# Two transformer blocks on one core: linear attention of the mixed layers by chunks, some low weight parts on GpSimd, a second buffer for the last gate parts

## The chip, the cores and the metric

One core of one Trainium2 chip runs the whole program. The metric is the device time of one execution in microseconds (us); lower is better. The kernel is given as instructions for each engine: TensorE (PE in the profile), VectorE (DVE), ScalarE (ACT), GpSimd (POOL) and SyncE (SP), which wait for each other on semaphores.

## The reference

A first block of two layers is followed by a second of four. Both work on 256 tokens of width 1024 in float32. The change touches the first block's mixed layers, and the end of every feed-forward stage. A layer of the first block is, cut to what matters:

```
x = x + 0.5 * gt1 * swiglu(norm(x))            # d_ff 2816
proj = norm(x) @ mix_w_in                       # a_q a_k a_v | b_u | c_q c_k c_v c_r c_g
o_a = attention(rope(norm(a_q)), rope(norm(a_k)), a_v)     # 8 heads of 64, causal
o_b = silu(layernorm(conv31(a * sigmoid(g))))              # 256 channels
log_decay = log_sigmoid(c_g @ gla_gate_w + gla_gate_b) / 16
o_c = norm(gla(c_q, c_k, c_v, log_decay)) * silu(c_r)      # 4 heads of 64
x = x + gt2 * (concat(o_a, o_b, o_c) @ mix_w_out)
x = x + 0.5 * gt3 * swiglu(norm(x))

def gla(q, k, v, g):        # chunks of 64 tokens, G = cumsum of g inside a chunk
    q_t, k_t = q / 8 * exp(G), k * exp(-G)
    o_intra  = tril(q_t k_t^T) v
    k_end    = k * exp(G_last - G)
    state_n  = exp(G_last) * state_(n-1) + k_end^T v
    return o_intra + q_t state_(n-1)
```

## The kernel before

**Weights.** All weights pass through four slots (`SLOTS`) of 2048 floats per partition, in the order of one list, `plan.stream`. A unit is 256 columns of a weight matrix. SP loads it into `raw`. ACT rounds it to a high part `whi` (line 767) once TensorE has released the slot. DVE subtracts and makes the low part `wlo` (line 1187). TensorE then does 48 matmuls of 256 columns with it, three products for each of 16 tiles. `ahead(pos)` in ACT's and DVE's programs makes the parts up to three units ahead of the unit named. SP reloads `raw` of a slot when both `hi_done` and `lo_done` of its last unit have come, and its loads are one queue in the order of the list. `LO_ON_DVE` names all four slots, so GpSimd has a memset of `gate_w` (line 746) and nothing else.

**Mixed layer.** `mix1` has 13 units: c_r, c_g, c_k, c_q, the two of the convolution, two of mq, two of mk, c_v, two of mv; below they are units 0 to 12. In the first layer unit 0 is in slot 2, so the units in slot 3, the fourth, are 1, 5 and 9; in the second layer unit 0 is in slot 3, so they are 0, 4, 8 and 12. After unit 2 TensorE multiplies the gate weights (L2137). DVE takes the minimum with 0 (L1587), ACT takes abs, exp and log (L942 to L948), DVE subtracts (L1592). DVE then goes through the remaining units: it makes low parts, does the 62 taps of the convolution in lots of 10, 12, 12, 12 (L1560, L1563), normalizes queries and keys (`scaled`, L1493) and applies the rotation (`rope`, L1575 to L1579). TensorE's group sum for a norm stands behind a unit (L2106), its rotation matmul (L2209) two units later. Rotation b of DVE waits for TensorE's matmul, which waits for `scaled` of b.

**Head loop.** After the last rotation all engines go through steps j = 0 to 10. In step j TensorE computes the scores of head j (L2166, L2167), transposes the probabilities of head j-2 (L1880) and multiplies those of head j-3 with the values (L2125, L2126). DVE adds the mask and takes the row maxima of head j (L1632 to L1635), divides head j-1 (L1499 to L1643) and, in steps 4, 6, 8, 10, makes the low part of a pair of heads (L1649) once ACT has made the high part (L981). ACT does the exponentials (L930) and copies the transposed rows (L975). In the same steps linear attention goes up a tree of nine levels: DVE multiplies queries and keys by decays (`up`, L1508 to L1521), TensorE multiplies them (`level`, L2120), DVE keeps the entries that belong to the level (`keep_level`, L1538, L1542) in `c_A`. Steps 0 to 3 also hold the last 16 taps. Step 4 has the convolution's mean (L2188), step 6 its variance (L2192), steps 7 to 10 its root, silu and parts. Behind the loop TensorE multiplies `c_A` with c_v, ACT squares, TensorE sums (L2106), ACT takes the root, DVE scales and gates, ACT and DVE make the parts of tiles 6 and 7. The output projection (`outp`, L2426) waits, in its first unit, for each of the eight tiles of its input in turn.

**Feed-forward.** Eight stages of eleven steps. A step's gated product is split by ACT into `ghi` (L866) and by DVE into `glo` (L1403, or L1393 in the second block), and TensorE multiplies them with the output weights (L2058; those of the last step at L2091). There is one `ghi` and one `glo`:

```
if st.uses[O1] + j > 0:
    act.wait_ge(used[O1], st.uses[O1] + j)
f(ghi[:, :, :], product, ACT.Copy).then_inc(q["ffn_hi"], 1)
```

so ACT waits until TensorE has done the output products of the step before.

Of the kernel before, what the change touches and what calls it, by code (L numbers as in the profile page):

```python
# [29 lines left out]
P = 128  # L30
D = 1024
KT = D // P
S = 256
# [17 lines left out]
LO_ON_DVE = (0, 1, 2, 3)  # L51
# [183 lines left out]
def build(nc, a, out):  # L235

    ctx = ExitStack()
    with ctx:
# [51 lines left out]
        def work(at, *dims):  # L290
# [35 lines left out]
        c_g, conv_sig = conv_sq[:, 0:256], conv_y  # L326

# [35 lines left out]
            "level_mm level_up level_cp tree_mm tree_out tree_hi tree_lo "  # L363
            "lower_done mix_f sgu_v sgu_s sgu_mm sgu_hi sgu_lo final_x final_mm final_c out_done").split()}
# [3 lines left out]
        class Lane:  # L368
# [5 lines left out]

            def at(self, i, name):
                return self.sem, i * len(self.steps) + self.steps.index(name) + 1
# [3 lines left out]
                   "inv e0 e1 lb_a lb lb_rest")  # L380
        FIRST_ROWS = ("c", "ffn1_norm", "ada_b0")
# [49 lines left out]

        stages.append(Stage(kind="prologue"))
# [3 lines left out]
        for l in range(DEPTH1):  # L436
# [10 lines left out]
            last_use[0] = units[-1]  # L447
            stages.append(Stage(kind="mix1", l=l, units=units, last=units[-1], gn=take("gn", 5), heads=take("heads", 8),
                                masked=take("masked", 8), pairs=take("pairs", 4), tree=take("tree"),
                                rope=take("rope", 4)))  # L450
# [79 lines left out]
        n_stream = len(plan.stream)  # L530

# [55 lines left out]
        def mixer_tile(st, k):  # L587

            m = st.mixer
            if m.kind == "mix1":  # L590
                if k >= 6:
                    return q["tree_lo"], tree_base(m.tree) + 1
# [152 lines left out]
        def _(pool):  # L745
            nc.gpsimd.memset(gate_w[96:128, :, :], 0.0).then_inc(q["pro_s"], 1)
            for s, use, _, size in plan.stream:
                if s in LO_ON_DVE:
                    continue

                pool.wait_ge(hi_done[s], use + 1)
                if use > 0:
                    pool.wait_ge(used[s], use)
                nc.gpsimd.tensor_tensor(wlo[:, s, 0:size], raw[:, s, 0:size], whi[:, s, 0:size].bitcast(F32),
                                        ALU.subtract).then_inc(lo_done[s], 1)


        @block_.scalar
        def _(act):
# [173 lines left out]
            def mix1(st):  # L933
                us = st.units
                GA = 4 * st.l
                for n, u in enumerate(us):
                    take_out(u)
                    if n == 5:
# [11 lines left out]
                        f(c_f, gate_min, ACT.Exp, scale=1.0 / TAU).then_inc(q["gate_s"], 1)  # L950
# [11 lines left out]
                for j in range(8 + 3):  # L962
# [36 lines left out]
                act.wait_ge(q["tree_mm"], tree_base(st.tree) + 1)  # L999
                square(st.gn + 4, ps[:, 7, :], m_sq)  # L1000
                root(st.gn + 4, 4, HD, m_rs)
                act.wait_ge(q["tree_out"], tree_base(st.tree) + 1)
                f(hhi[:, 6:8, :], m_t[:, 0, :], ACT.Copy).then_inc(q["tree_hi"], 1)
# [172 lines left out]
        def _(dve):  # L1176
# [3 lines left out]
            def take_lo(s, use, size):  # L1180
                if s not in LO_ON_DVE:
                    return

# [183 lines left out]
            def ffn(st):  # L1367
                lo0 = STEPS * st.i
                A, B, _, O1 = st.slots
                for j in range(STEPS):  # L1370
                    pa, pb, o0, o1 = ffn_pos(st, j)
                    ahead(pb if st.defer is None else pa)
                    if st.defer is not None:
# [19 lines left out]
                        tt(glo[:, :, :], product, ghi[:, :, :].bitcast(F32), ALU.subtract).then_inc(q["ffn_lo"], 1)  # L1393
# [9 lines left out]
                    tt(glo[:, :, :], product, ghi[:, :, :].bitcast(F32), ALU.subtract).then_inc(q["ffn_lo"], 1)  # L1403
# [141 lines left out]
            def mix1(st):  # L1545
# [34 lines left out]

                for n, u in enumerate(us):
                    take_out(u)
                    if n == 4:
# [877 lines left out]
```

## Time and profile before

| | us |
|---|---|
| three runs | 2851.28, 2853.35, 2855.09 |
| median | 2853.35 |
| the profiled execution's own time | 2852.6 |
| its span, first to last instruction | 2850.8 |
| TensorE busy in the span | 2707.0 (95%) |
| VectorE busy | 1890.2 (66%) |
| ScalarE busy | 1343.5 (47%) |
| GpSimd busy | 0.7 |
| granted TensorE clock, mean | 0.976 |

Busy time is a sum over the span; the wait that a change removes or adds is found where one engine stands and another works. For this kernel these are the two mixed layers (about 290 to 433 and 860 to 1003 us of the span) and the ends of the eight feed-forward stages. A granted clock of 0.5 is 1.2 GHz and one of 1.0 is 2.4 GHz.

### The profile page before, as it was taken

How to read it: one execution, taken by the hardware profiler on the slowest of the kernel's cores; microseconds unless marked ns; L12 is line 12 of the kernel's file. 1: busy time of each engine (PE TensorE's matmuls, PEld its weight loads, DVE VectorE, ACT ScalarE, POOL GpSimd, SP SyncE). 2: the span in 40 equal slices, each digit the busy share in tenths (PEclk: the TensorE clock that was granted, in tenths of full speed). 3: DMA queues.
4: the chain of work that ended last, by engine and by line, in shares of the span. 5: the costliest groups of instructions: out<-in, count | busy, mean ns of one | idle time of the engine just before them, and what ended most of it. 6: DMA issues, size and time to landing. Idle time of an engine off the chain costs nothing.

```text
span 2850.8 us, 53332 instructions
## 1 busy us (share of the span) xinstructions
PE 2707.0 (95%) x22439; PEld 2628.3 (92%) x22439; DVE 1890.2 (66%) x2639; ACT 1343.5 (47%) x1576; POOL 0.7 (0%) x5
## 2 busy tenths in 40 slices
PE   6799979999999799999999999999999999999998
PEld 6799959999999599999999999999999999999998
DVE  5877786877777855576565666656566555775564
ACT  3334634435446354465544535544465544555443
POOL 0000000000000000000000000000000000000000
PEclk8899979999999799999999999999999999999999
DMA  8988505997985045664355643535665266643552
GB/s 238 310 287 276 170 27 185 296 291 266 290 287 172 21 144 196 206 193 149 104 200 184 197 152 109 163 133 193 206 206 178 104 207 199 201 147 118 178 192 103
DMA packets 458802, 533.07 MB, mean 187 GB/s; under 512 B 9879, under 2 KB 435081, under 8 KB 458633
## 3 DMA queue, kind: packets, MB, share of 16 engines
q1 hardware_dynamic: 457340, 530.11, 56.9%
q8 instruction: 113, 1.85, 0.3%
q10 hardware_dynamic: 1293, 0.65, 0.1%
q14 instruction: 56, 0.46, 0.0%
HBM read 528.10 MB, written 2.62 MB: 186 GB/s over the span
## 4 chain that ended last, share of the span: by engine, by line
PE 79%; DVE 10%; DMA 3%; issue 3%; ACT 3%; SPq 1%; ACTq 0%; DVEq 0%
PE ps L2058 13%; PE ps L1889 11%; PE ps L1890 11%; PE ps L1891 11%; PE ps L1907 10%; PE ps L2426 8%; DMA work<-in_ada_w 3%; DVE work L1291 2%; DVE wlo L1187 2%; PE ps L2091 2%; DVE work L1563 2%; PE ps L2120 1%; PE ps L2236 1%; PE ps L2238 1%; PE ps L2237 1%
## 5 line engine op out<-in xcount | busy, mean ns | idle before, releaser
L1187 DVE TENSOR_TENSOR wlo<-raw,whi 128x2048 fp32r<-128x2048 f32 (+1 forms) x514 | 975.8, 1919 | 410.2 <-ACT whi L767 410.0
L767 ACT ACTIVATE whi<-raw 128x2048 fp32r<-128x2048 f32 (+1 forms) x514 | 826.4, 1615 | 436.5 <-PE ps L1891 148.0
L1889 PE MATMUL ps<-hhi,whi 128*128 128x256 f32 x1600 | 451.4, 282 | 13.8 <-issue 11.1
L1890 PE MATMUL ps<-hlo,whi 128*128 128x256 f32 x1600 | 445.0, 278 | 0.0
L1891 PE MATMUL ps<-hhi,wlo 128*128 128x256 f32 x1600 | 444.4, 278 | 0.0
L1889 PE MATMUL ps<-parts_f,whi 128*128 128x256 f32 x1344 | 372.6, 277 | 7.8 <-issue 7.8
L1890 PE MATMUL ps<-parts_f,whi 128*128 128x256 f32 x1344 | 371.5, 276 | 0.0
L1891 PE MATMUL ps<-parts_f,wlo 128*128 128x256 f32 x1344 | 371.2, 276 | 0.0
L2058 PE MATMUL ps<-ghi,whi 128*128 128x256 f32 x1280 | 355.5, 278 | 7.1 <-DVE wlo L1187 7.0
L2058 PE MATMUL ps<-glo,whi 128*128 128x256 f32 x1280 | 355.2, 278 | 0.0
L2058 PE MATMUL ps<-ghi,wlo 128*128 128x256 f32 x1280 | 354.9, 277 | 0.0
L1889 PEld LDWEIGHTS ps<-hhi,whi 128*128 128x128 f32 x1600 | 303.2, 190 | 18.0 <-issue 18.0
L1890 PEld LDWEIGHTS ps<-hlo,whi 128*128 128x128 f32 x1600 | 303.4, 190 | 0.7 <-issue 0.7
L1891 PEld LDWEIGHTS ps<-hhi,wlo 128*128 128x128 f32 x1600 | 302.9, 189 | 0.0
L1889 PEld LDWEIGHTS ps<-parts_f,whi 128*128 128x128 f32 x1344 | 252.3, 188 | 9.3 <-issue 9.2
L1890 PEld LDWEIGHTS ps<-parts_f,whi 128*128 128x128 f32 x1344 | 252.3, 188 | 0.1
L1891 PEld LDWEIGHTS ps<-parts_f,wlo 128*128 128x128 f32 x1344 | 252.3, 188 | 0.0
L2058 PEld LDWEIGHTS ps<-ghi,whi 128*128 128x128 f32 x1280 | 241.5, 189 | 8.2 <-issue 8.2
L2058 PEld LDWEIGHTS ps<-glo,whi 128*128 128x128 f32 x1280 | 241.5, 189 | 0.0
L2058 PEld LDWEIGHTS ps<-ghi,wlo 128*128 128x128 f32 x1280 | 241.4, 189 | 0.0
L1291 DVE SCALAR_TENSOR_TENSOR work<-work,silu_c 128x256 f32<-128x256 f32 x490 | 197.0, 479 | 0.0
L1907 PE MATMUL ps<-hhi,whi 128*128 128x256 f32 x880 | 177.5, 284 | 16.2 <-DVE hlo L1352 16.2
(277 smaller groups left out, 4892.0 us busy)
## 6 DMA issues: line engine op xcount, KB each, us to landing
raw<-in_ffn_w_in SPq DMA_DIRECT2D x88, 1024.0 KB, 10.6
raw<-in_ffn_w_gu SPq DMA_DIRECT2D x88, 1024.0 KB, 5.1
work<-in_ada_w SPq DMA_DIRECT2D x72, 1024.0 KB, 8.9
raw<-in_ffn_w_out SPq DMA_DIRECT2D x88, 512.0 KB, 6.0
raw<-in_ffn_w_down SPq DMA_DIRECT2D x88, 512.0 KB, 5.4
raw<-in_ca_w_kv SPq DMA_DIRECT2D x32, 1024.0 KB, 5.8
raw<-in_mix_w_in SPq DMA_DIRECT2D x24, 1024.0 KB, 6.3
raw<-in_da_w_in SPq DMA_DIRECT2D x24, 1024.0 KB, 6.0
```

The lines of the kernel that those rows point to most:

```text
L767: f(whi[:, s, 0:size], raw[:, s, 0:size], ACT.Copy).then_inc(hi_done[s], 1)
L1187: tt(wlo[:, s, 0:size], raw[:, s, 0:size], whi[:, s, 0:size].bitcast(F32), ALU.subtract).then_inc(lo_done[s], 1)
L1291: m = stt(acc, w, silu_c[:, k:k + 1], acc, ALU.mult, ALU.add)
L1563: m = stt(conv_acc[:, t, :], h, w, conv_acc[:, t, :], ALU.mult, ALU.add)
L1889: mm(dst, wh, xh, start=first, stop=False)
L1890: mm(dst, wh, xl, start=False, stop=False)
L1891: return mm(dst, wl, xh, start=False, stop=last)
L1907: o = mm(ps[:, slot, 256 * m:256 * m + 256], w[:, k, P * m:P * m + P], x_[:, k, :], start=k == 0 and i == 0 and m == 0, stop=k == KT - 1 a ...
L2058: o = mm(dst, a_, b_[:, t, :], start=first and t == 0 and i == 0 and m % 2 == 0, stop=False, skip_group_check=True)
L2091: o = mm(dst, a_, b_[:, t, :], start=False, stop=t == 1 and i == 2 and m % 2 == 1, skip_group_check=True)
L2120: o = mm(d[:, c], K[rows_, tile, c], Q[rows_, tile, c], start=True, stop=True)
L2426: o = mm(ps[:, bank, 256 * m:256 * m + 256], w[:, k, P * m:P * m + P], x_[:, k, :], start=k == 0 and i == 0 and m == 0, stop=k == KT - 1 a ...
```

## The change

Linear attention in `mix1` no longer uses the tree. DVE makes three masks out of constants (five small operations, in `rstd`), sums the log decays inside chunks of 64 tokens with two scans, and ACT takes exp of the sums and of their negatives (one more exp than before). DVE multiplies queries and keys (three operations of 128x512 and one small copy in `decayed`; two of 128x128 in `far`). TensorE multiplies in three rounds (`gla_level` 0, 1, 2) in steps 0, 1, 2 of the head loop, in place of nine, and DVE keeps what belongs in `c_A` in the same steps. `c_A` is cleared by GpSimd first. The product with c_v moves to step 4, the square to ACT's step 5, the group sum to TensorE's step 6, the root to ACT's step 7, scaling and gating to DVE's step 8; the parts of tiles 6 and 7 come last. The second block's tree (`hgrn`) is as before but for the numbering of its semaphore.

GpSimd makes the low parts of the units that `mix1` has in slot 3. The gate parts of the last step of each feed-forward stage go to `parts_f`, and ACT does not wait for TensorE there.

```diff
-LO_ON_DVE = (0, 1, 2, 3)
+POOL_SLOT = 3
...
+        gate_sum, decay_in, growth_in, k_end = c_f, gate_abs, gate_min, c_f
+        reset, intra = rstd[:, 1, :], rstd[:, 0, 0:P]
+        decay = stat[:, :, 12:16]
...
+        GLA = Lane("gla_v", "ones reset below within intra sums q_in k_in decay k_end q_far k_far")
...
+            pool_units.append([u for u in units if u.slot == POOL_SLOT])
...
+        def gate_parts(j):
+
+            return (ghi[:, :, :], glo[:, :, :]) if j < STEPS - 1 else (fhi[:, 0:2, :], flo[:, 0:2, :])
...
+            for l in range(DEPTH1):
+                for n, u in enumerate(pool_units[l]):
+                    take_lo(u.slot, u.use, KT * u.cols)
+                    if n == 1:
+                        pool.wait_ge(*GLA.at(l, "k_end"))
+                        nc.gpsimd.memset(c_A, 0.0).then_inc(q["gla_zero"], 1)
...
-                    if st.uses[O1] + j > 0:
+                    if j < STEPS - 1 and st.uses[O1] + j > 0:
                         act.wait_ge(used[O1], st.uses[O1] + j)
-                    f(ghi[:, :, :], product, ACT.Copy).then_inc(q["ffn_hi"], 1)
+                    f(gate_parts(j)[0], product, ACT.Copy).then_inc(q["ffn_hi"], 1)
...
-                        f(c_f, gate_min, ACT.Exp, scale=1.0 / TAU).then_inc(q["gate_s"], 1)
+                        act.wait_ge(*GLA.at(st.l, "sums"))
+                        f(decay_in, gate_sum, ACT.Exp, scale=1.0 / TAU).then_inc(q["gla_s"], 1)
+                        f(growth_in, gate_sum, ACT.Exp, scale=-1.0 / TAU).then_inc(q["gla_s"], 1)
...
                     if j == 5:
+                        act.wait_ge(q["gla_tokens"], st.l + 1)
+                        square(st.gn + 4, ps[:, 1, :], m_sq)
...
                     if j == 7:
+                        root(st.gn + 4, 2, HD, m_rs)
...
+                def decayed():
+
+                    dve.wait_ge(q["gla_s"], 2 * l + 2)
+                    for u in us[2:4]:
+                        dve.wait_ge(*bank_read(u))
+                    tt(c_q, c_q, decay_in, ALU.mult).then_inc(*GLA.step)
+                    tt(c_k, c_k, growth_in, ALU.mult).then_inc(*GLA.step)
+                    v.tensor_copy(decay, decay_in[:, :, HD - 1::HD]).then_inc(*GLA.step)
+                    dve.wait_ge(*GLA.at(l, "k_in"))
+                    last = chunks(decay_in)[:, :, HD - 1:HD].broadcast_to([P, 8, HD])
+                    tt(chunks(k_end), chunks(c_k), last, ALU.mult).then_inc(*GLA.step)
...
+                    if n == 1:
+                        masks()
+                    if n == 6:
+                        decayed()
...
+                        for t in range(2):
+                            m = v.tensor_tensor_scan(gate_sum[:, t, :], reset, gate_min[:, t, :], 0.0, ALU.mult, ALU.add)
+                        m.then_inc(*GLA.step)
...
-                    if j < LEVELS:
-                        keep_level(st.tree, j, c_A, 4, source)
+                    if j < 3:
+                        keep(j)
+                    if j == 1:
+                        far()
...
-                        level(st.tree, j, c_q, c_k, 4, dst, part)
+                    if j < 3:
+                        gla_level(j)
                     if j == 4:
+                        gla_tokens()
```

Three places show how the instructions now stand. First VectorE in the second mixed layer, from the end of the gates to the first rotation; `work` holds all activations of the stage. Before:

```order
L1592 TENSOR_TENSOR work<-work 128x512
L1187 TENSOR_TENSOR wlo<-raw,whi 128x2048
L1594 MEMSET work 128x2x30
L1597 TENSOR_TENSOR work<-ps,work 128x2x256
L1560 TENSOR_SCALAR work<-work,taps,vec 128x256 x2
L1563 SCALAR_TENSOR_TENSOR work<-work,taps 128x256 x8
L1187 TENSOR_TENSOR wlo<-raw,whi 128x2048 x3
L1493 SCALAR_TENSOR_TENSOR work<-ps,lam,work 128x512
L1563 SCALAR_TENSOR_TENSOR work<-work,taps 128x256 x12
L1187 TENSOR_TENSOR wlo<-raw,whi 128x2048
```

Now:

```order
L1675 TENSOR_TENSOR work<-work 128x512
L1679 SCALAR_TENSOR_TENSOR work<-rstd,work 128x256 x2
L1682 MEMSET work 128x2x30
L1685 TENSOR_TENSOR work<-ps,work 128x2x256
L1583 TENSOR_SCALAR work<-work,taps,vec 128x256 x2
L1586 SCALAR_TENSOR_TENSOR work<-work,taps 128x256 x8
L1208 TENSOR_TENSOR wlo<-raw,whi 128x2048
L1625 TENSOR_TENSOR work<-work 128x512
L1626 TENSOR_TENSOR work<-work 128x512
L1627 COPY stat<-work 128x2x4
L1630 TENSOR_TENSOR work<-work 128x512
L1208 TENSOR_TENSOR wlo<-raw,whi 128x2048 x2
```

The scans (L1679) and the four operations of `decayed` (L1625 to L1630, the last is k_end) have come in, and two low parts, of units 8 and 12, have left this stretch.

Second, GpSimd from its old memset on, both layers:

```order
L761 MEMSET gate_w 32x512
L767 ISA
L767 TENSOR_TENSOR wlo<-raw,whi 128x1024
L767 TENSOR_TENSOR wlo<-raw,whi 128x2048
L775 MEMSET work 128x1536
L767 TENSOR_TENSOR wlo<-raw,whi 128x2048 x3
L775 MEMSET work 128x1536
L767 TENSOR_TENSOR wlo<-raw,whi 128x2048 x2
```

The memset of `c_A`, which waits for k_end, stands ahead of the low part of unit 9 in the first layer and ahead of those of units 8 and 12 in the second.

Third, TensorE in step 4 of the head loop, after the scores, with the products of head 1's values, then of c_v, then the convolution's mean (L2290):

```order
L2206 MATMUL ps<-work 64x256
L2207 MATMUL ps<-work 64x128
L2206 MATMUL ps<-work 64x256
L2207 MATMUL ps<-work 64x128
L2206 MATMUL ps<-work 64x256
L2207 MATMUL ps<-work 64x128
L2206 MATMUL ps<-work 64x256
L2207 MATMUL ps<-work 64x128
L2206 MATMUL ps<-work 64x256
L2207 MATMUL ps<-work 64x128
L2290 MATMUL ps<-work,con 128x512
```

The last four pairs ahead of L2290 are those of c_v, which stood behind the whole loop before.

## Rows read from the trace of the kernel before

**Rows 1.** Page, part 1: busy time, share of the span, instructions

```profile
PE 2707.0 (95%) x22439; PEld 2628.3 (92%) x22439; DVE 1890.2 (66%) x2639; ACT 1343.5 (47%) x1576; POOL 0.7 (0%) x5
```

**Rows 2.** Busy time by stretch: PE, PEld, DVE, ACT, POOL, PEclk, DMA share, GB/s

```profile
322.00:371.00 49.00, 42.51 (x321) 38.12 (x320) 48.07 (x75) 22.79 (x22) 0.00 (x0) 0.97 0.47 151
371.00:432.00 61.00, 46.19 (x283) 32.98 (x283) 45.75 (x134) 22.11 (x57) 0.00 (x0) 0.75 0.00 1
...
941.00:1000.00 59.00, 45.02 (x270) 32.55 (x271) 44.69 (x133) 21.75 (x57) 0.00 (x0) 0.74 0.00 1
```

**Rows 3.** Waits of TensorE, 942 to 1003 us: total us, times, longest; line 2120

```profile
PE ps L2120 <- DVE work L1518: 7.2, 6, 1.9
```

**Rows 4.** Waits of TensorE over the whole span, those of line 2091

```profile
PE ps L2091 <- DVE glo L1393: 6.0, 4, 1.5
PE ps L2091 <- DVE glo L1403: 3.7, 4, 1.5
```

**Rows 5.** Timeline, end of the fourth feed-forward stage: start, us, engine, [idle before]

```profile
1202.54 0.63 ACT L866 ACTIVATE ghi<-work 128x512 fp32r<-128x512 f32 x1 [4.39 <-PE ps L2058]
...
1203.95 0.38 PE L2091 MATMUL ps<-ghi,whi 128*128 128x256 f32 x1 [1.51 <-DVE glo L1403]
```

**Rows 6.** Timeline of DVE in the second mixed layer, after the gates

```profile
892.01 0.69 DVE L1592 TENSOR_TENSOR work<-work 128x512 f32<-128x512 f32 x1 [9.63 <-ACT work L948]
892.62 2.29 DVE L1187 TENSOR_TENSOR wlo<-raw,whi 128x2048 fp32r<-128x2048 f32 x1
894.87 0.11 DVE L1594 MEMSET work<- 128x60 f32 x1
...
899.38 6.70 DVE L1187 TENSOR_TENSOR wlo<-raw,whi 128x2048 fp32r<-128x2048 f32 x3
```

**Rows 7.** The instructions that write the gate weights: min/median/max ns, first and last start

```profile
L746 POOL MEMSET gate_w<- x1: 520/520/520, 0.7 to 0.7; 32x512 f32 x1
```

**Rows 8.** Timeline of PE and DVE around the first rotation, second mixed layer

```profile
898.43 1.02 PE L2106 MATMUL ps<-work,con 128*128 128x512 f32 x2
...
912.03 1.02 PE L2209 MATMUL ps<-work,con 128*128 128x512 f32 x2
...
914.26 0.70 DVE L1575 TENSOR_TENSOR work<-ps,cs 128x512 f32<-128x512 f32 x1
```

**Rows 9.** The same in the first mixed layer

```profile
335.58 1.02 PE L2106 MATMUL ps<-work,con 128*128 128x512 f32 x2
...
342.82 1.02 PE L2209 MATMUL ps<-work,con 128*128 128x512 f32 x2
...
345.03 0.69 DVE L1575 TENSOR_TENSOR work<-ps,cs 128x512 f32<-128x512 f32 x1
```

**Rows 10.** Timeline of DVE in the head loop, first mixed layer

```profile
373.85 0.56 DVE L1632 TENSOR_TENSOR work<-ps,con 128x384 f32<-128x384 f32 x1 [1.80 <-PE ps L2167]
...
381.71 1.44 DVE L1542 COPY_PREDICATED work<-con,ps 128x256 f32<-128x256 int32 x4 [0.62 <-PE ps L2120]
383.05 1.66 DVE L1563 SCALAR_TENSOR_TENSOR work<-work,taps 128x256 f32<-128x256 f32 x4
...
397.72 0.55 DVE L1632 TENSOR_TENSOR work<-ps,con 128x384 f32<-128x384 f32 x1
...
399.23 0.35 DVE L1643 TENSOR_SCALAR work<-work,stat 128x256 f32<-128x256 f32 x1
...
421.88 0.87 DVE L1662 SCALAR_TENSOR_TENSOR work<-work,vec 128x256 f32<-128x256 f32 x2
```

**Rows 11.** Timeline of PE in the loop and behind it, first mixed layer

```profile
399.79 2.07 PE L2188 MATMUL ps<-work,con 128*128 128x512 f32 x2
...
426.48 1.13 PE L2106 MATMUL ps<-work,con 128*128 128x512 f32 x2 [2.83 <-ACT work L916]
...
431.96 0.51 PE L2426 MATMUL ps<-hhi,whi 128*128 128x256 f32 x2 [0.25 <-DVE hlo L1675]
```

**Rows 12.** Stretch in which the second output projection starts (columns as in rows 2)

```profile
995.00:999.00 4.00, 4.00 (x18) 3.49 (x18) 1.73 (x3) 1.41 (x3) 0.00 (x0) 0.59 0.01 4
```

More of the change, by code:

```diff
@@ L373, in __init__, with step @@
                 self.sem, self.steps = q[name], steps.split()
+            @property
+            def step(self):
+                return self.sem, 1
             def at(self, i, name):
@@ L530, in build @@
         n_stream = len(plan.stream)
+        on_pool = {(u.slot, u.use) for units in pool_units for u in units}
         def all_read(units):
@@ L746, in _, with take_lo @@
             nc.gpsimd.memset(gate_w[96:128, :, :], 0.0).then_inc(q["pro_s"], 1)
-            for s, use, _, size in plan.stream:
-                if s in LO_ON_DVE:
-                    continue
+            def take_lo(s, use, size):
                 pool.wait_ge(hi_done[s], use + 1)
@@ L934, in mix1 @@
                 us = st.units
[L935 removed]
+                GA = 3 * st.l
                 for n, u in enumerate(us):
@@ L997, in mix1 @@
                         f(hhi[:, 4:6, :], conv_y, ACT.Copy).then_inc(q["conv_hi"], 1)
[L999 to L1003, printed above, removed]
+                act.wait_ge(q["gla_out"], st.l + 1)
+                f(hhi[:, 6:8, :], m_t[:, 0, :], ACT.Copy).then_inc(q["gla_hi"], 1)
             def diff(st):
@@ L1180, in take_lo @@
             def take_lo(s, use, size):
-                if s not in LO_ON_DVE:
+                if (s, use) in on_pool:
                     return
@@ L1579, in rope, with masks @@
                     tt(dst, rows2(t), rows2(m_rope), ALU.add).then_inc(q["rope_done"], 1)
+                def masks():
+                    tril = const("tril")
+                    v.memset(rstd[:, 1, :], 1.0).then_inc(*GLA.step)
+                    dve.wait_ge(*GLA.at(l, "ones"))
+                    v.memset(rstd[:, 1, 0::HD], 0.0).then_inc(*GLA.step)
+                    tt(intra, block, tril, ALU.mult).then_inc(*GLA.step)
+                    dve.wait_ge(*GLA.at(l, "below"))
+                    tt(intra, block, intra, ALU.subtract).then_inc(*GLA.step)
+                    dve.wait_ge(*GLA.at(l, "within"))
+                    tt(intra, intra, ident, ALU.add).then_inc(*GLA.step)
@@ new lines, in far, with keep @@
+                def far():
+                    dve.wait_ge(q["gla_mm"], 3 * l + 2)
+                    dve.wait_ge(*GLA.at(l, "k_end"))
+                    tt(c_q[:, :, 3 * HD:], c_q[:, :, 3 * HD:], decay[:, :, 2:3].broadcast_to([P, 2, HD]), ALU.mult)\
+                        .then_inc(*GLA.step)
+                    tt(k_end[:, :, 0:HD], k_end[:, :, 0:HD], decay[:, :, 1:2].broadcast_to([P, 2, HD]), ALU.mult)\
+                        .then_inc(*GLA.step)
+                def keep(L):
+                    dve.wait_ge(q["gla_mm"], 3 * l + L + 1)
+                    if L:
+                        dve.wait_ge(q["gla_cp"], 3 * l + L)
+                    else:
+                        dve.wait_ge(q["gla_zero"], l + 1)
+                        dve.wait_ge(*GLA.at(l, "intra"))
+                    far_level = const("level")[:, 6 * P:7 * P]
+                    for h in range(4):
+                        src = ps[:, (1, 2)[h % 2], 256 * (h // 2):256 * (h // 2) + 256]
+                        if L == 2:
+                            m = v.tensor_copy(c_A[:, h, P:2 * P], src[:, 0:P])
+                            continue
+                        dst = c_A[:, h, :].rearrange("p (c t) -> p c t", c=3)[:, 0::2, :]
+                        mask = (intra, far_level)[L].bitcast(I32).unsqueeze(1).broadcast_to([P, 2, P])
+                        m = v.copy_predicated(dst, mask, rows2(src))
+                    m.then_inc(q["gla_cp"], 1)
```

85 lines of the change are left out of this document (48 added, 37 removed).

## The prediction

> **What bounds the kernel now.** I read the busy shares first: TensorE is busy 2707 of 2850.8 us [rows 1], so some 144 us of standing still are all that a change of order can win, and only where TensorE stands. The busy time by stretch then shows where. In the mixed layers' unit stretch DVE is busy 48.07 of 49 us while TensorE is at 42.5; in the head loop behind it TensorE is busy 46.2 of 61 us, and its clock is granted at 0.75, a mix of the two levels [rows 2]. The reader is to see that DVE sets the pace in both. TensorE's waits name what ends last in the loop: the levels of the tree wait for DVE's multiplication of the keys (L1518), 7.2 us in one layer [rows 3]. The same view of the whole span has one more regular wait, at the last gate parts: 6.0 + 3.7 us over the eight feed-forward stages [rows 4]. About 0.2%, 5.7 us, is what a measurement of this kernel can tell from no change.
>
> **The change part by part.**
>
> *Last gate parts.* TensorE ends a stage's tenth output products, ACT then rounds (0.63), DVE subtracts (0.69), and TensorE has stood 1.51 us [rows 5]. With a second buffer both are done while TensorE works on the tenth step's outputs. The product is there by then, since it needs only the last input products. The eight waits are 9.7 us [rows 4]; where low parts or ada sums occupy DVE before, the shorter wait shows it. The next thing late is the low part of the last output unit, which DVE has made before those waits end. **-9.7**, bounds -7 and -9.7.
>
> *Gates to k_end, on DVE.* Second layer: the subtraction starts at 892.01 and ends 0.69 later, 892.7 [rows 6]. Two scans of 256: no row has one. Bounds are 0.4 each (a tap, a quarter of 1.66 [rows 10]) and twice that; I take 0.6, since each element waits for the one before: 893.9. The low part of unit 8 (2.2) goes to GpSimd. Memset, gating and ten taps are 894.87 to 899.38 [rows 6], 4.5: 898.4. Low part of unit 9, 2.2: 900.6. Three multiplications at 0.6 (the 0.69 of rows 6 less overlap) and a copy, 2.1: **k_end at 902.7**. First layer: the subtraction starts at 322.8 (as far ahead of the rotation, 345.03 less 914.26 - 892.01, [rows 8, 9]) and unit 8's low part is still on DVE: k_end at 333.5. ACT's extra exp (0.63) is covered by DVE's gating and taps, and the five mask operations stand where DVE idles 9.63 us ahead of the subtraction [rows 6].
>
> *GpSimd.* Behind k_end comes the memset of 1536 elements. The only row is 512 elements in 0.52 us [rows 7]: 1.5 us. Then the low part that TensorE wants next. A subtraction on GpSimd has no row. Lower bound 2.29, DVE's own time [rows 6]; upper bound 6.3, two reads and a write of 2048 each at the memset's pace of 1 ns. I take the middle, **4.3**. So unit 8 of the second layer has its low part at 902.7 + 1.5 + 4.3 = 908.5, and unit 9 of the first at 333.5 + 5.8 = 339.3. (The Trainium skill, GPSIMD Engine Reference, Elementwise side-by-side cycle accounting, gives 4497 ns for this size against 2293 ns on VectorE; by its figure each layer would be 0.2 us later. The trace agrees on VectorE's.) The earlier units in slot 3 are made long before their use, in DVE's idle time.
>
> *What that wait does.* TensorE wants unit 8 when the group sum of 898.43 is through, at 899.0, so it stands 9.5 us. From there the rotation ends at 913.05 and DVE uses it at 914.26 [rows 8]. After the stall the clock starts low; I add 1.6, what the 4 us at 0.59 in rows 12 lose. The rotation ends at 913.05 + 9.5 + 1.6 = 924.2, so DVE's chain is **9.9 late**. It was the chain that ended last, and the low part of unit 12 that it no longer makes stood before this point, so it gives nothing back. First layer: unit 9 is wanted at 336.2, the stall is 3.1, the rotation of 343.84 comes at 346.9, against 345.03 [rows 9]: **1.9 late**; DVE by itself (+1.2 scans, +2.1 multiplications, -2.2 for unit 9) would be 1.1 late. Queued behind: SP's load of the next slot-3 unit waits for GpSimd, and three loads behind it. They have over 12 us until TensorE frees their slots, with DMA at 0.47 [rows 2]; nothing.
>
> *Head loop, first layer as the example.* Steps 0 to 3 ran from 373.85 to 397.72, 23.9 us [rows 10]. DVE now has in them a softmax part of 1.86 (397.72 to 399.58) three times and 1.2 once, 6.8; four lots of taps at 1.66, 6.6; two keeps at 1.44 and one of half that, 3.6 [rows 10]; two small multiplications, 0.6: 17.6, **-6.3**. TensorE's share is shorter. Steps 4 to 8, 397.72 to 421.88, 24.2 us, were not paced by DVE alone, but by the round from probabilities over TensorE and ACT to the pair's low part. Gone are five levels with their waits, 5 of the 7.2 us [rows 3]. New on TensorE are c_v's products and the group sum. The mean's product, 512 columns, is 2.07 at the low clock [rows 11], so the group sum is 2.1 and c_v's 1536 columns 3.1 to 6.2; lower if a pair's heads run side by side, which I take. New on ACT are a square and a root, 1.9. That is 7.1 against 5 and the levels' own matmuls: **0**, bounds -6 and +7. Behind step 8 the time from 421.88 to 431.96 plus two tiles of 0.68 was 11.4 [rows 10, 11], with the group sum waiting 2.83 for ACT. Now it is the convolution's scale, silu, table, parts, then five tiles: 0.9 + 0.9 + 1.3 + 0.6 + 0.4 + 0.4, some 4.9 with waits, + 3.4 + 1.6 for a low clock [rows 12] = 9.9, **-1.5**. Sum -7.8; for the waits between engines I take **-7 a layer**, bounds -3 and -10.
>
> *Sum.* -9.7 + 1.9 + 9.9 - 14 = -11.9. The profiled execution took 2852.6, its span being 2850.8; that gives 2840.7. The median stands 0.75 above that execution: **2841.5 us**.
>
> **Rivals.**
>
> *DVE held (2847).* While GpSimd subtracts, DVE's own operations with two inputs in SBUF stand. No row shows the two engines working together, so bounds are nothing and a whole GpSimd instruction. In the first layer GpSimd's 4.3 us fall on low parts and taps, so the chain is 5.6 late, not 1.9: +3.7. In the second the subtraction of unit 8 waits for one of DVE's (+0.7) and that of unit 12 takes DVE up to 1.5 more: +2. Against it: most of its time in the second layer DVE would wait for TensorE anyway. (The Trainium skill, SBUF, Who interferes with whom, states this rule: a VectorE instruction with two SBUF inputs and a GpSimd one that reads SBUF exclude each other for the whole instruction. The trace has nothing to weigh it.)
>
> *GpSimd starved: slower (2863).* The same exclusion, but DVE's queue is never empty (48.07 of 49 us [rows 2]) and keeps going first. GpSimd starts only where DVE stops, at the first rotation. First layer: DVE has 12.7 us of work after 333.5 (three low parts at 2.2, twelve taps 4.8, two scalings 1.3), so 346.2 + 4.3, unit 9 at 350.5, rotation at 350.5 + 7.6 + 1.6 = 359.7, 14.7 late. Second (two low parts): 913.3 + 4.3 = 917.6, rotation 14.1 + 1.6 later, 933.3, 19.0 late. Together 33.7 in place of 11.8: +21.9. It turns the sign when GpSimd starts over 9 us late in each layer.
>
> *Low clock throughout (2850).* With less for TensorE in the loop the clock may stay at 1.2 GHz for steps 4 to 8 and the projection. Only about 3 a layer would be left: +8. For it: 0.75 and 0.74 now [rows 2]. Against: the matmuls of steps 2 to 5 close up.
>
> *The gate parts bring nothing (2851).* If the low part of the last output unit, or DVE's ada sums, end as late: +9.7.
>
> *The stall is not there (2833).* A memset and a subtraction at DVE's pace, 3 us together, give back 2.8 in the second layer and 1 in the first, and with DVE short of work the loop may give 10: -9 in all.
>
> **How the numbers follow.** Forecast 0.42, held 0.25, low clock 0.10, starved 0.10, gates nothing 0.07, no stall 0.06. Faster by over 0.2% means below 2847.6: nearly all of the forecast (0.39), over half of held (0.14), a little of low clock (0.02), all of no stall: 0.61. Slower is starved: 0.10. Same: 0.29. The range leaves out starved and half of no stall: 2834 to 2851, which also takes in the bounds of the scan, the subtraction and the loop.
>
> **What would show it.** Eight gaps before the last outputs (L2091's successor) shrink from 1.5 to near zero. TensorE waits once for GpSimd's `wlo`, 9 to 10 us in the second mixed layer and about 3 in the first. The GpSimd subtraction reads 4 to 5 us. From the first rotation to the loop nothing changes; steps 0 to 3 take 17 to 18 us, steps 4 to 8 about 24. DVE's taps and low parts keep their 0.4 and 2.29 us; if one of them reads 4 us or more, DVE was held. Wrong would be a GpSimd subtraction that starts over 5 us after its memset, or a loop with no shorter steps.

## The result and the profile after

The changed kernel takes **2837.99 us** (median of 4 runs, 2835.5 to 2838.6) against 2854.22 for the kernel before on the same chip (4 runs): ratio 0.994, 95% interval 0.9924 to 0.9956. The forecast was 2841.5 in 2834 to 2851, so the sign held and the time lies 3.5 us below it. The profiled execution took 2838.55 us and its span is 2836.7, 14.1 less than before; the forecast's sum was -11.9.

The page's busy times, against [rows 1]: TensorE 9.3 us less, DVE 15.6 less, GpSimd 35.6 in place of 0.7.

```profile
PE 2697.7 (95%) x22247; PEld 2615.3 (92%) x22247; DVE 1874.6 (66%) x2568; ACT 1343.6 (47%) x1578; POOL 35.6 (1%) x14
```

I laid the two traces side by side at the first operation of each norm. The span's 14.1 us come from: -1.9 in the start, +2.3 in the first feed-forward stage, **-5.4 in the first mixed layer**, +1.1 and -2.6 in the next two feed-forward stages, **+3.0 in the second mixed layer**, **-9.4 in the five later feed-forward stages** (-1.96, -1.79, -2.06, -1.81, -1.78), and -1.1 spread over the rest. The first two are no work of the change: other kernels below, which differ little up to there, stand anywhere from 3.0 us ahead of the kernel before (kernel 3, end of the start) to 3.2 behind it (kernel 9, end of the first stage).

Within the mixed layers the same marks in both kernels, taken from the timelines (us; "rotation" is the first use of a rotated head pair on DVE, L1575 before and L1598 after):

| stretch | before, layer 1 / 2 | after, layer 1 / 2 | difference | forecast |
|---|---|---|---|---|
| norm to gate subtraction | 40.19 / 40.22 | 39.38 / 40.16 | -0.8 / -0.1 | 0 |
| gate subtraction to first rotation | 22.24 / 22.25 | 27.61 / 32.70 | **+5.4 / +10.4** | +1.9 / +9.9 |
| first rotation to step 0 | 28.82 / 28.98 | 28.80 / 28.91 | 0 / -0.1 | 0 |
| steps 0 to 3 | 23.87 / 23.83 | 17.35 / 17.36 | **-6.5 / -6.5** | -6.3 |
| step 4 to the convolution's scale | 24.16 / 23.10 | 24.22 / 25.15 | +0.1 / +2.1 | 0 |
| from there to the next norm | 31.54 / 32.67 | 28.08 / 29.73 | **-3.5 / -2.9** | -1.5 |

**GpSimd.** Its timeline around the gates, first layer and then second:

```profile
299.96 4.79 POOL L767 TENSOR_TENSOR wlo<-raw,whi 128x2048 fp32r<-128x2048 f32 x1 [22.65 <-ACT whi L787]
333.04 1.39 POOL L775 MEMSET work<- 128x1536 f32 x1 [28.29 <-DVE work L1630]
334.39 5.20 POOL L767 TENSOR_TENSOR wlo<-raw,whi 128x2048 fp32r<-128x2048 f32 x1
...
896.10 1.38 POOL L775 MEMSET work<- 128x1536 f32 x1 [31.29 <-DVE work L1630]
897.44 5.16 POOL L767 TENSOR_TENSOR wlo<-raw,whi 128x2048 fp32r<-128x2048 f32 x1
```

DVE in the same places:

```profile
300.62 4.29 DVE L1610 TENSOR_TENSOR rstd<-con 128x128 f32<-128x128 f32 x1
...
332.29 0.69 DVE L1630 TENSOR_TENSOR work<-work 128x512 f32<-128x512 f32 x1
332.90 8.84 DVE L1208 TENSOR_TENSOR wlo<-raw,whi 128x2048 fp32r<-128x2048 f32 x2
...
349.93 0.67 DVE L1598 TENSOR_TENSOR work<-ps,cs 128x512 f32<-128x512 f32 x1
...
859.40 0.28 DVE L1610 TENSOR_TENSOR rstd<-con 128x128 f32<-128x128 f32 x1
...
885.36 0.69 DVE L1675 TENSOR_TENSOR work<-work 128x512 f32<-128x512 f32 x1 [9.63 <-ACT work L968]
886.08 1.27 DVE L1679 TENSOR_TENSOR_SCAN work<-rstd,work 128x256 f32<-128x256 f32 x2
...
895.35 0.69 DVE L1630 TENSOR_TENSOR work<-work 128x512 f32<-128x512 f32 x1
895.96 8.78 DVE L1208 TENSOR_TENSOR wlo<-raw,whi 128x2048 fp32r<-128x2048 f32 x2
...
918.06 0.69 DVE L1598 TENSOR_TENSOR work<-ps,cs 128x512 f32<-128x512 f32 x1 [4.02 <-PE ps L2304]
```

The reader is to see L1610 twice: 0.28 us where GpSimd is idle, 4.29 where GpSimd subtracts; and two low parts at 8.8 us that take 4.5 elsewhere. DVE was held. The order can be read too: GpSimd's subtraction takes 4.60 us when alone, but 5.16 to 5.20 behind DVE's low part. It waits for the running one (895.96 + 2.2 = 898.2, less 897.44), works 4.6 us, which together is 0.2 more than was read, and DVE's next starts when it is done. Each lets the other in after one instruction, so neither starves.

TensorE's timeline at the two units in question, first layer and then second:

```profile
336.19 1.02 PE L2187 MATMUL ps<-work,con 128*128 128x512 f32 x2
339.69 0.77 PE L1987 MATMUL ps<-hhi,whi 128*128 128x256 f32 x2 [2.47 <-issue]
...
892.84 1.10 PE L2187 MATMUL ps<-work,con 128*128 128x512 f32 x2 [0.91 <-ACT work L936]
902.70 0.76 PE L1987 MATMUL ps<-hhi,whi 128*128 128x256 f32 x2 [8.76 <-issue]
```

Both resume 0.1 us behind the end of GpSimd's subtraction (334.39 + 5.20, 897.44 + 5.16), though the view calls the wait "issue".

**The loop.** The stretches of the loop (columns as in [rows 2]): the first layer's steps 0 to 3 and its steps 4 to 8, then the second layer's:

```profile
378.73:396.08 17.35, 15.18 (x73) 10.43 (x74) 16.44 (x52) 5.42 (x19) 0.00 (x0) 0.50 0.00 1
396.08:420.30 24.22, 18.25 (x77) 9.78 (x73) 9.47 (x32) 10.76 (x31) 0.00 (x0) 0.83 0.00 0
...
946.97:964.33 17.36, 15.18 (x73) 10.43 (x74) 16.44 (x51) 5.41 (x19) 0.00 (x0) 0.50 0.00 1
964.33:989.48 25.15, 21.09 (x77) 11.15 (x73) 9.47 (x32) 10.77 (x31) 0.00 (x0) 0.67 0.00 0
```

DVE works 16.4 of the 17.4 us of steps 0 to 3 and stands for 15 of 25 us behind them. Steps 4 to 8 took longer where the granted clock stayed low: 0.67 and 25.2 us, against 0.83 and 24.2.

**The gate parts.** TensorE's waits at the last outputs are gone: in none of the eight stages does it stand before them. At the end of the fourth feed-forward stage, where it stood 1.51 us [rows 5], its timeline now reads:

```profile
1198.42 0.28 PE L2138 MATMUL ps<-ghi,wlo 128*128 128x256 f32 x1
1198.54 0.39 PE L2172 MATMUL ps<-parts_f,whi 128*128 128x256 f32 x2
```

DVE's timeline there in the kernel before (the last gate product is the first row):

```profile
1197.08 0.69 DVE L1400 TENSOR_TENSOR work<-work,ps 128x512 f32<-128x512 f32 x1 [2.69 <-PE ps L1891]
...
1205.01 2.29 DVE L1187 TENSOR_TENSOR wlo<-raw,whi 128x2048 fp32r<-128x2048 f32 x1 [1.11 <-ACT whi L767]
...
1207.42 3.23 DVE L1438 SCALAR_TENSOR_TENSOR x<-ps,scale_out,x 128x256 f32<-128x256 f32 x8
```

The same in the changed kernel:

```profile
1193.34 0.69 DVE L1422 TENSOR_TENSOR work<-work,ps 128x512 f32<-128x512 f32 x1 [2.69 <-PE ps L1971]
...
1198.03 2.29 DVE L1208 TENSOR_TENSOR wlo<-raw,whi 128x2048 fp32r<-128x2048 f32 x1 [1.77 <-ACT whi L787]
...
1200.44 1.89 DVE L1461 SCALAR_TENSOR_TENSOR x<-ps,scale_out,x 128x256 f32<-128x256 f32 x4
1202.82 0.88 DVE L1461 SCALAR_TENSOR_TENSOR x<-ps,scale_out,x 128x256 f32<-128x256 f32 x2 [0.48 <-PE ps L2172]
1204.18 0.88 DVE L1461 SCALAR_TENSOR_TENSOR x<-ps,scale_out,x 128x256 f32<-128x256 f32 x2 [0.48 <-PE ps L2172]
```

Before, all eight updates of x ran back to back: they were late, behind a low part that was late because ACT rounded its unit only after the gate parts (1202.54 in [rows 5]). Now the last four wait for TensorE. From gate product to last update it was 1210.65 - 1197.08 = 13.57 us, and is 1205.06 - 1193.34 = 11.72: 1.85 won, not 1.51.

### The profile page after: what moved, and what is told of

Its sections match the earlier page's. It is cut to its first block, busy times and chain, and to the rows that moved or that the text cites. A ratio compares the mean times of both kernels' runs of the same rounds, so it can differ in the third digit from the quotient of the medians.

```text
span 2836.7 us, 52845 instructions
## 1 busy us (share of the span) xinstructions
PE 2697.7 (95%) x22247; PEld 2615.3 (92%) x22247; DVE 1874.6 (66%) x2568; ACT 1343.6 (47%) x1578; POOL 35.6 (1%) x14
## 4 chain that ended last, share of the span: by engine, by line
PE 81%; DVE 8%; DMA 4%; issue 3%; ACT 3%; SPq 0%; ACTq 0%; DVEq 0%
PE ps L2138 14%; PE ps L1969 12%; PE ps L1970 11%; PE ps L1971 11%; PE ps L1987 10%; PE ps L2522 8%; DMA work<-in_ada_w 2%; DVE work L1312 2%; DVE wlo L1208 2%; PE ps L2172 2%; PE ps L2331 1%; PE ps L2333 1%; PE ps L2332 1%; DMA bias_rows<-raw 1%; DVE work L1586 1%
## 5 line engine op out<-in xcount | busy, mean ns | idle before, releaser
L1969 PE MATMUL ps<-hhi,whi 128*128 128x256 f32 x1600 | 452.1, 283 | 16.2 <-issue 14.2
L1987 PE MATMUL ps<-hhi,whi 128*128 128x256 f32 x880 | 178.9, 285 | 27.5 <-DVE hlo L1373 16.3
```

What stands on the lines that cost most here:

```text
L1969: mm(dst, wh, xh, start=first, stop=False)
L1987: o = mm(ps[:, slot, 256 * m:256 * m + 256], w[:, k, P * m:P * m + P], x_[:, k, :], start=k == 0 and i == 0 and m == 0, stop=k == KT - 1 a ...
```

## The experiments

All are compared with the kernel before, run beside them on the same chip. Stretches are from each kernel's profiled execution.

**1. The gate parts alone.** The kernel before with the second buffer:

```diff
+ def gate_parts(j): return (ghi, glo) if j < STEPS - 1 else (fhi[:, 0:2, :], flo[:, 0:2, :])
- if st.uses[O1] + j > 0:
+ if j < STEPS - 1 and st.uses[O1] + j > 0:
      act.wait_ge(used[O1], st.uses[O1] + j)
- f(ghi[:, :, :], product, ACT.Copy).then_inc(q["ffn_hi"], 1)
+ f(gate_parts(j)[0], product, ACT.Copy).then_inc(q["ffn_hi"], 1)
...
```

> The kernel before with the second buffer for the last gate parts and nothing else. Theory Q (the queue behind): in the fourth feed-forward stage the time from the last gate product on DVE to the last update of x fell from 13.57 us (1197.08 to 1210.65) to 11.72 us (1193.34 to 1205.06), 1.85 and not 1.51, because ACT's rounding of the gate parts no longer delays the two weight units behind it, whose low part stands in DVE's queue ahead of the updates of x. Eight stages at 1.85: -14.8, about 2839.4. Rival W (only TensorE's waits, as forecast): -9.7, about 2844.5. A third, that stages with ada sums gain less than the others because DVE is busy there anyway: between 2840 and 2846 with the later five at 1.8 to 2.0 and the first three below 1.

Measured: 2843.71 us (2836.7 to 2846.12) against 2854.96, ratio 0.9956 (0.9941 to 0.997): -11.3. The five later feed-forward stages gave -1.93, -1.78, -2.05, -1.81 and -2.03; the fourth as much as in the changed kernel. Of the three stages with ada sums (TensorE's products with `in_ada_w`, which make `mods`) the second gave -0.8 and the third -0.1; over eight of the profiles with the second buffer (kernels 1, 2, 4, 7 to 10 and the changed kernel) they average 0.0 and -1.6, against +0.2 and -0.3 in the one other kernel without it. The first can't be told from the start's variation. By the total (the interval is -8.6 to -16.8 us) W and the third theory can't be told apart; by the stages the third holds for the five later ones, 1.9 each. What the first three give is known less well: some 1 to 1.6 us in the second and third together, on average all of it in the third.

One more thing stands in this profile. Its tree is the old one, and yet steps 4 to 8 of its head loop took 28.24 us in the first layer and 22.25 in the second, where the kernel before took 24.16 and 23.10 (columns as in [rows 2]):

```profile
395.90:424.14 28.24, 25.54 (x127) 16.48 (x127) 19.06 (x64) 9.32 (x28) 0.00 (x0) 0.64 0.00 1
970.47:992.72 22.25, 16.82 (x127) 11.01 (x127) 18.78 (x63) 9.43 (x28) 0.00 (x0) 1.00 0.00 1
```

So the same instructions took 6 us more in one layer than in the other, at a lower granted clock.

**2. All low parts on DVE.**

```diff
- pool_units.append([u for u in units if u.slot == POOL_SLOT])
+ pool_units.append([])
...
```

GpSimd's memset of the score tile stays; with no units left it stands alone.

> The changed kernel with every low part on DVE; GpSimd keeps only the memset of the score tile. Theory G (GpSimd's low parts are late themselves and hold DVE): the first rotation comes 22.2 + 1.3 (scans) + 2.1 (multiplications) = 25.6 us behind the gate subtraction in both layers, against 27.6 and 32.7 in the changed kernel, so -2.0 and -7.1: about 2829. DVE's mask multiplication reads 0.28 us in both layers and two low parts 4.5. Rival L (the loop sets the time and takes back what comes earlier, by a lower clock or the later rotation): less than 3 us faster, 2835 to 2838. Rival D (DVE's three low parts more per layer, 6.9 us, fall on the chain): 2 to 7 us slower than the changed kernel.

Measured: **2829.03 us** (2826.91 to 2832.24), ratio 0.9911 (0.9894 to 0.9929). Gate subtraction to rotation is 25.45 and 25.46 us, where 25.6 was expected. The mask multiplication reads 0.28, two low parts 4.49. GpSimd's part in the change was a loss of 2.2 and 7.2 us ahead of the rotation. Rivals L and D fall.

**3. Linear attention by chunks alone.** Kernel 2 with the last gate parts in the old buffer.

> Linear attention by chunks alone: low parts all on DVE, last gate parts in the one buffer as before. By parts against the kernel before: +3.4 a layer ahead of the first rotation (scans 1.3, multiplications 2.1), -6.3 in the loop's steps 0 to 3, 0 in steps 4 to 8, -1.5 (forecast) to -3.4 (read in the changed kernel's first layer) behind it: -8.8 to -12.6 for two layers, 2841.5 to 2845.5. With theory Q it should stand 14.8 above low_on_dve, with W 9.7. A rival in which the earlier rotation only makes a longer wait in the loop: 2849 or more.

Measured: 2838.68 us (2834.07 to 2844.18), ratio 0.9946 (0.9926 to 0.9966): -16.3, more than the sum by parts. In its profile the two mixed layers give -7.6 and -7.0, the start -3.0 and the first feed-forward stage +1.6. Stretches: rotation at 25.46 in both layers, steps 0 to 3 17.4, steps 4 to 8 22.0 and 24.0, then 28.1 twice (before 31.5 and 32.7): the sum by parts is passed behind the loop and, by 2 us, in steps 4 to 8 of the first layer. It stands 9.7 above kernel 2. That is W's number, but not by W's parts: in the two profiles the five later stages alone differ by 9.7. With the 11.3 of kernel 1 that makes some 10 us for the gate parts.

**4. The memset behind the third low part.**

```diff
- if n == 1:
+ if n == 2:
      pool.wait_ge(*GLA.at(l, "k_end"))
      nc.gpsimd.memset(c_A, 0.0).then_inc(q["gla_zero"], 1)
```

> The changed kernel with one line moved: GpSimd makes its third low part of a layer as soon as ACT has rounded the unit, and the memset of the score tile, which waits for the decayed keys, comes behind it and not ahead. It tells the late start from the hold. Theory G: TensorE's stall of 8.76 us in the second layer is gone, DVE is still held for 4.3 us, so its chain is 25.6 - 2.3 (a low part less) + 4.3 = 27.6 us long in both layers, against 27.6 and 32.7: -5, about 2833. If the hold cost nothing, 23.3 in both: -4.3 and -9.4, about 2824. If the late start cost nothing (the hold alone): no change, 2838. In the trace one of DVE's operations with two inputs beside GpSimd's subtraction should read 4 us more than its usual time.

Measured: 2830.43 us (2825.87 to 2834.36), ratio 0.9914 (0.9895 to 0.9934). GpSimd's timeline around the gates:

```profile
327.31 4.59 POOL L767 TENSOR_TENSOR wlo<-raw,whi 128x2048 fp32r<-128x2048 f32 x1 [23.52 <-ACT whi L787]
...
875.27 4.62 POOL L767 TENSOR_TENSOR wlo<-raw,whi 128x2048 fp32r<-128x2048 f32 x1 [12.16 <-ACT whi L787]
...
899.13 4.82 POOL L767 TENSOR_TENSOR wlo<-raw,whi 128x2048 fp32r<-128x2048 f32 x1 [4.06 <-ACT whi L787]
```

DVE's operations beside the first and the last of them:

```profile
327.00 5.05 DVE L1583 TENSOR_SCALAR work<-work,taps,vec 128x256 f32<-128x256 f32 x2
...
898.60 9.20 DVE L1586 SCALAR_TENSOR_TENSOR work<-work,taps 128x256 f32<-128x256 f32 x12
```

This run parts the two mechanisms. In the first layer the part is made in time for TensorE, yet the rotation comes at 27.58 us, as in the changed kernel: there the hold alone is the cost (two taps 5.05 us in place of 0.74). In the second the late start was: the part is now made at 875.27, while DVE stands ahead of the gates, the stall is gone, and the rotation comes at 25.45, not 32.70 nor my 27.6. I had not seen that the part falls into DVE's idle time; of two low parts less (-4.5) and one hold (+4.4, twelve taps 9.20 in place of 4.83) nothing is left.

**5 and 6. What in GpSimd's instruction holds DVE.** Its subtraction is replaced. In place of the fourth slot's low part kernel 5 has a copy of the whole unit and kernel 6 zeros, so neither computes what the kernel should; they are for the timelines alone.

```diff
- nc.gpsimd.tensor_tensor(wlo[:, s, 0:size], raw[:, s, 0:size], whi[:, s, 0:size].bitcast(F32), ALU.subtract)
+ nc.gpsimd.tensor_copy(wlo[:, s, 0:size], raw[:, s, 0:size])
```

in kernel 5, and in kernel 6

```diff
+ nc.gpsimd.memset(wlo[:, s, 0:size].bitcast(F32), 0.0)
```

> The changed kernel with GpSimd's subtraction replaced by a copy of the unit (one input from SBUF in place of two; the low parts of the fourth slot are left out of the products). Theory R (what holds DVE is that GpSimd reads SBUF while DVE has two inputs there): DVE is still held, for as long as the copy takes; the mask multiplication in the first layer (0.28 us by itself, 4.29 beside the subtraction) reads over 1 us, and one of the two low parts behind the decayed keys waits for the copy's whole length. Theory T (only a GpSimd instruction with two inputs holds): 0.28 us and 4.5 us for the two.

> The changed kernel with GpSimd's subtraction replaced by a memset of the same 2048 elements (nothing read; the low parts of the fourth slot are left out). Theory R: DVE is not held; the mask multiplication reads 0.28 us in both layers and the two low parts behind the decayed keys 4.5 us. A rival in which any GpSimd access of SBUF holds DVE: some of them read 1.5 to 2 us more. The memset of 1536 elements took 1.38 us, so 2048 should take 1.8; TensorE's stall at the third unit of the second layer falls by 3 to 7 us, from 8.76, the rest being the wait for the decayed keys.

Kernel 5 (2837.09 us, one run), GpSimd's timeline:

```profile
302.13 2.11 POOL L767 CAST wlo<-raw 128x2048 fp32r<-128x2048 f32 x1 [22.82 <-ACT whi L786]
...
336.61 2.57 POOL L767 CAST wlo<-raw 128x2048 fp32r<-128x2048 f32 x1
```

DVE's in the same places:

```profile
302.80 1.58 DVE L1609 TENSOR_TENSOR rstd<-con 128x128 f32<-128x128 f32 x1
...
335.13 6.19 DVE L1207 TENSOR_TENSOR wlo<-raw,whi 128x2048 fp32r<-128x2048 f32 x2
```

Kernel 6 (2827.44 us, one run), GpSimd's timeline:

```profile
299.63 1.81 POOL L767 MEMSET wlo<- 128x2048 f32 x1 [24.92 <-ACT whi L786]
...
334.07 1.83 POOL L767 MEMSET wlo<- 128x2048 f32 x1
```

And DVE's:

```profile
300.31 0.29 DVE L1609 TENSOR_TENSOR rstd<-con 128x128 f32<-128x128 f32 x1
...
332.60 4.49 DVE L1207 TENSOR_TENSOR wlo<-raw,whi 128x2048 fp32r<-128x2048 f32 x2
```

For DVE's operations with two inputs theory R holds: a copy of 1.9 us holds the next one (+1.3, +1.7 us), a memset of 1.8 us over the same time does not (0.29, 4.49). It is GpSimd's read that counts there, one input being enough. In kernel 6 the first rotation of the first layer stands at 23.3 us. In the second it is at 29.3: the unit is released only at 890.24 + 1.81, since the memset of the score tile still waits for the decayed keys. That is the late start without any hold.

**7. GpSimd only where DVE is idle.** The fourth slot's first two units of the first layer, its first three of the second, the memset behind them.

```diff
- pool_units.append([u for u in units if u.slot == POOL_SLOT])
+ pool_units.append([u for u in units if u.slot == POOL_SLOT][:2 + l])
```

> GpSimd makes low parts only where DVE stands idle: the first two units of the fourth slot in both layers and the third of the second layer (ahead of the gates), the memset behind them; the rest on DVE. Theory G: TensorE never waits for GpSimd, DVE has one low part less (2.3 us) between the gates and the first rotation of the second layer, 23.2 us against 25.5 with all of them on DVE, and 25.5 in the first: 2 us faster than low_on_dve. Rival L (what comes earlier is lost in the loop): the same as low_on_dve within 1 us.

Measured: 2824.77 us (2823.46 to 2826.12), ratio 0.9901 (0.9884 to 0.9918). Rotations at 25.47 and 23.29 us, as expected. That 2.2 us shows in the profile; the ratio's interval overlaps kernel 2's, so by their times the two can't be told apart.

**8. The linear attention three steps later.** Kernel 2 with the decayed keys out of the unit stretch:

```diff
- if n == 6:
-     decayed()
...
- if j < 3:
-     keep(j)
+ if j == 2:
+     decayed()
+ if 3 <= j < 6:
+     keep(j - 3)
...
```

> low_on_dve with the linear attention three steps later in the head loop: decayed keys at DVE's step 2 and not in the unit stretch, levels at steps 3, 4 and 5, the sum over tokens at 6, square at 7, root at 8, gating at 9. DVE works without a pause from the gates to step 4 and then stands for 16 of 25 us, so what crosses step 4 (keeps 1.44 + 0.7, two small multiplications 0.6: 2.7 us) is won if DVE sets the pace up to step 4 and has slack behind it: 25.5 + 28.8 + 17.4 = 71.7 us from the gate subtraction to step 4 become 69.0, and steps 4 to 8 stay at 22 to 25 us: 5 us faster than low_on_dve over two layers. Rival P (behind step 4 TensorE is the bound, busy 21.2 of 25.3 us at a granted clock of 0.66, and the level products now fall there): 69.0 all the same, but steps 4 to 8 3 us longer: no change.

Measured: **2817.70 us** (2814.49 to 2818.17), ratio **0.9872** (0.9852 to 0.9893), 20 us below the changed kernel. Steps 0 to 3 and 4 to 8 of the first layer's loop as windows (columns as in [rows 2]), kernel 2:

```profile
375.00:392.36 17.36, 13.89 (x73) 9.60 (x74) 16.45 (x52) 5.42 (x19) 0.00 (x0) 0.60 0.00 1
392.36:417.72 25.36, 21.27 (x76) 11.24 (x73) 9.47 (x32) 10.75 (x31) 0.00 (x0) 0.66 0.00 0
```

Kernel 8:

```profile
374.05:390.07 16.02, 11.84 (x62) 7.88 (x61) 15.77 (x45) 5.42 (x19) 1.38 (x1) 0.61 0.00 1
390.07:411.70 21.63, 15.89 (x79) 9.06 (x80) 11.81 (x42) 9.92 (x29) 0.00 (x0) 0.89 0.00 0
```

Gate subtraction to step 4 fell from 71.6 to 68.4 us (expected 69.0), since DVE sets that pace: 6.5 us over two layers. Steps 4 to 8 fell too, from 25.4 and 23.9 to 21.6 and 22.0, in the first layer at a granted clock of 0.89 in place of 0.66, TensorE doing more matmuls (79 against 76) in less busy time. Rival P falls. These other 5.6 us were not expected, and why the clock came back earlier isn't settled by this run. They are hardly chance: the four readings of kernels 8 and 9 are 21.6 to 22.0, the sixteen of the kernels that have linear attention in its old place 22.0 to 25.4. The stretch behind step 8 grew by 2.4 over the two layers (29.3 and 30.9, against 29.8 and 28.1).

**9 and 10. Both together, and the changed kernel beside it.**

> late3 and pool_idle together: linear attention three steps later, GpSimd's low parts where DVE stands idle. Theory G: the first rotation comes 23.5 us behind the gate subtraction in the first layer (as late3) and 23.5 - 2.2 = 21.3 in the second (a low part less, nothing held), the loop as in late3: 2 us below late3, about 2815.5, and 22 below the changed kernel. Rival: with DVE that much earlier the first rotation of the second layer waits for TensorE and the gain stops short, 22.5 to 23.5 us: the same as late3.

> The changed kernel itself, unaltered, on the chip and in the rounds of late3_idle, so that the two stand side by side: 2838 against the kernel before at 2854, ratio 0.994 to 0.996. In its trace the two mixed layers should read again 27.6 and 32.7 us from the gate subtraction to the first rotation and 17.4 us for steps 0 to 3; steps 4 to 8 may vary by 2 us with the granted clock.

Measured: 2819.44 us (2818.95 to 2821.83), ratio 0.9876 (0.9858 to 0.9895), and for the changed kernel 2840.02 (2838.72 to 2846.05), ratio 0.9952 (0.9934 to 0.997), both against 2855.66. The changed kernel repeats: 27.61 and 32.67 us to the rotation, steps 0 to 3 17.4. Kernel 9 has its rotations at 23.54 and 22.22: of the 2.2 us that one low part less should give only 1.3 came, since DVE then waits 0.8 us for TensorE's rotation matmul. That is the rival's mechanism, of which less came than it had (22.5 to 23.5), and the time is kernel 8's. Kernels 8 and 9 can't be told apart; both beat the kernel before and the change.

## Why the prediction was right, and where it was not

*Last gate parts* (-9.7). The waits of TensorE went as told, the sum is nearly right: 11.3 by the run alone, 9.7 by the pair of kernels 2 and 3. The failed sentence is "The next thing late is the low part of the last output unit, which DVE has made before those waits end". What was late stood behind: ACT's roundings of the next stage's units and the low part ahead of the updates of x. Five stages give 1.9, not 1.5. The three with ada sums, whose waits in [rows 4] share 3.7 - 1.5 = 2.2 us, lost these waits too, but on average the second shows no gain and the third 1.6, and what the first gains can't be read. That the sum fits is in part luck: 2 too little in five stages against some too much in three.

*Gates to k_end.* Right: scans 1.27 for two (taken 1.2); the keys' multiplication ends 895.35 + 0.69 - 885.36 = 10.7 us behind the subtraction, as in the sum. Memset 1.38 (1.5), GpSimd's subtraction 4.6 by itself (4.3), 5.2 behind DVE.

*GpSimd and what its wait does.* The second layer's stall came nearly as told, 8.76 us (9.5), and the rotation 10.4 late (9.9). In the first layer the step that failed is "the rotation comes 1.9 late": DVE's own chain was taken as free (1.1 late by itself), and the hold added 4.3 to it. The rotation came 5.4 late, the rival *DVE held* having 5.6 (its own terms, 1.1 + 4.3, give 5.4); its condition, DVE operations with two inputs of 4 us and more, is met. The runs without the hold (2, 8) and with nothing but the hold (4, first layer) show it. (The Trainium skill, SBUF, Who interferes with whom, states the rule, and the trace agrees: held beside a subtraction and a copy, not beside a memset.) So this rival was true as a mechanism with a chance of 0.25, and its 3.7 us in the first layer were paid; of its 2 us in the second 0.5 came. Its time, 2847, didn't come because the terms behind the loop were too cautious and the start ran 1.9 us shorter.

*Starved* is refuted: GpSimd started within one DVE instruction of its memset.

*Head loop.* Steps 0 to 3 -6.5 (forecast -6.3). Steps 4 to 8 +0.1 and +2.1 (0): of *low clock* the second layer shows a part, 25.2 us at 0.67. Over all profiles with linear attention by chunks at its place they take 22.0 to 25.4 us, whatever else the kernel does, and with the old tree 22.3 to 28.2 (kernel 1, kernel before). The 2.1 us are within that variation, so no run shows them to be the change's. Behind step 8 the mis-sized term: -1.5 was 11.4 less 9.9, with 1.6 for a low clock. The first layer had full clock there and ended at 8.0 (-3.5); the second, which had some of it, -2.9. All other parts of the 9.9 were right: 4.57 us to the last five tiles, taken 4.9.

*Sum.* By the profiled executions: gates -8.7 (-9.7), first layer -5.4 (-5.1), second +3.0 (+2.9), the rest -3.0 (0), of which -1.9 is the start's variation. (The gates' -8.7 holds the first stage's +2.3, which is variation too.) That the two layers fit within 0.3 us is luck, since errors cancelled. In the first it was 3.5 too little delay, against 2.0 too little gain behind the loop, 0.8 ahead of the gates and the 0.8 that I had rounded off the loop's sum. In the second it was 2.1 in steps 4 to 8 and 0.5 at the rotation, against 1.4 behind the loop, the 0.8 and 0.3 elsewhere. The medians differ by 16.2 and, in the second pair, by 15.6, the profiled spans by 14.1 and 13.9; the 2 us between are the spread of single executions.

## What to carry to other kernels

Work given to GpSimd is not free beside a busy DVE. Here a GpSimd subtraction cost a busy DVE nearly its whole length (4.3 of 4.6 us, for 2.2 us of work taken off it), so hand over only what falls into DVE's idle time. In an in-order queue see what a wait for something else (here a memset's, for the keys) puts ahead of the piece that TensorE needs next. When an engine sets the pace up to a point and idles behind it, moving work over that point pays: three steps' delay of the linear attention, with no work saved, won some 10 us on top of kernel 2's 26. Of these 6.5 are the work moved; the rest, faster steps 4 to 8 less a longer stretch behind them, has no shown cause.

## What was not expected of the hardware

- One GpSimd instruction with a single input holds DVE's operations with two inputs as well (+1.3 and +1.7 us beside a copy of 1.9 to 2.6), one without input doesn't.
- DVE's TENSOR_SCALAR, with one tensor and two scalars per partition in SBUF, was held too: two in 5.05 us in place of 0.74 (kernel 4). Its scalars in SBUF aren't needed for that: L1451 multiplies one small tensor by the constant 0.5 and takes 0.17 us by itself, but in the changed kernel, beside GpSimd's subtraction from 834.71 to 839.31,

```profile
836.39 2.95 DVE L1451 TENSOR_SCALAR scale_out<-mods 128x8 f32<-128x8 f32 x1
```

  Beside kernel 6's memset the same instruction once read 0.32 us and ended with it, so for this form a GpSimd instruction without input may hold as well; one reading doesn't show it.
- An operation with one of its two tensors in PSUM was not held: L1516, reading `ps`, took 0.75 us at 913.29, beside GpSimd's subtraction of 912.02, as it does elsewhere (0.74).
- Beside each other the engines alternate by whole instructions; in no profile does either wait for two.
- The same stretch of TensorE work with low duty, steps 4 to 8, takes 22.0 to 25.4 us in kernels that don't differ there, with a granted clock of 0.66 and 0.67 in the long ones shown and 0.83 where they took 24.2, and 22.3 to 28.2 us with the old tree; a gain of 2 us behind such a stretch needs the profile of stretches, not the total.
